# Start addresses of a float32r matmul kernel's moving tiles, modulo 256 bytes

## What is computed

```python
def _ffn_half(h, g, shift, scale, gate, w_in, w_out):            # first block, d_ff = 2816
    a, b = jnp.split(_modnorm(h, g, shift, scale) @ w_in, 2, axis=-1)
    return h + 0.5 * gate * ((jax.nn.silu(a) * b) @ w_out)
...
q, k, v, g = _ret_project(u, w_in, rope)                         # retention: query, key, value, gate
...
def second_block(x, ...):                                        # two layers
        f = _swiglu(_rmsnorm_2(h, ff1_norm_pre[l]), ff1_w_gate[l], ff1_w_up[l], ff1_w_down[l])
        h = h + 0.5 * _rmsnorm_2(f, ff1_norm_post[l])
        m = _hybrid_mixer(_rmsnorm_2(h, mix_norm_pre[l]), w_in[l], ...)   # SSD, pooling, attention
        h = h + _rmsnorm_2(m, mix_norm_post[l])
        f = _swiglu(_rmsnorm_2(h, ff2_norm_pre[l]), ff2_w_gate[l], ff2_w_up[l], ff2_w_down[l])
        h = h + 0.5 * _rmsnorm_2(f, ff2_norm_post[l])
```

## The kernel before

| product | lines | columns | moving, block | distance |
|---|---|---|---|---|
| first block at 512 tokens | L1193 to L1195, L1201, L1202, L1208 | 512 | 128, 128 | 0 |
| its token halves | L1289, L1291, L1297, L1327 to L1329, L1193 to L1195 (Fourier output) | 256 | 128, 128 | 0 |
| query and gate of the retention | L1193 to L1195 | 256 | 128, 128 | 0 |
| values of the retention | L1224 | 256 | 64, 128 | 192 |
| Fourier products, retention output | L1818, L1831, L1193 to L1195 | 256 | 64, 128 | 192 |
| last feed-forward of the first block, second block | L1193 to L1195, L1201, L1202, L1208 | 256 | 64, 128 | 192 |
| attention values of the second block | L1224 | 256 | 64, 64 | 0 |
| pool columns of the second block | L1224 | 264 | 128, 160, 192 or 224, 64 | 64 to 160 |

## Time and profile before

### The profile page before, as it was taken

One profiled execution on the slowest core, in us unless ns is written; L12 is line 12 of the kernel. 1 busy time (PEld: TensorE's weight loads), 2 busy tenths in 40 slices (PEclk: granted clock), 3 DMA queues, 4 the chain that ended last, 5 costly groups with the idle time before them and its releaser, 6 DMA issues. The chain is left out here.

```text
span 2772.4 us, 45421 instructions
## 1 busy us (share of the span) xinstructions
PE 2693.6 (97%) x18884; PEld 2464.9 (89%) x18884; DVE 1700.0 (61%) x2148; ACT 1135.4 (41%) x1432; POOL 0.9 (0%) x13
## 2 busy tenths in 40 slices
PE   7999999999999999999999999999999999998998
PEld 5878898878889888899998999999889999997998
DVE  6774655776325753444456655766877666587764
ACT  5222234522224222235245544544555454454543
POOL 0000000000000000000000000000000000000000
PEclk9999999999999999999999999999999999999999
DMA  8653631466233663544222566575526656652563
GB/s 271 210 182 113 191 111 61 143 185 190 88 95 109 197 195 121 175 136 130 86 92 92 183 193 190 167 221 173 153 77 197 188 168 197 191 168 76 166 180 126
DMA packets 377437, 428.86 MB, mean 155 GB/s; under 512 B 14016, under 2 KB 359488, under 8 KB 377152
## 3 DMA queue, kind: packets, MB, share of 16 engines
q1 hardware_dynamic: 376416, 424.79, 49.9%
q10 hardware_dynamic: 864, 1.80, 0.2%
HBM read 425.49 MB, written 1.05 MB: 154 GB/s over the span
## 5 line engine op out<-in xcount | busy, mean ns | idle before, releaser
L736 DVE TENSOR_TENSOR w_lo<-raw,w_hi 128x1024 fp32r<-128x1024 f32 (+1 forms) x672 | 798.8, 1198 | 806.3 <-ACT w_hi L727 799.5
L727 ACT ACTIVATE w_hi<-raw 128x1024 fp32r<-128x1024 f32 (+1 forms) x672 | 691.1, 1036 | 1018.8 <-PE ps L1195 839.7
L1193 PE MATMUL ps<-u_hi,w_hi 128*128 128x256 f32 (+1 forms) x3168 | 1000.8, 316 | 9.4 <-DVE tmp L1137 4.0
L1195 PE MATMUL ps<-u_hi,w_lo 128*128 128x256 f32 (+1 forms) x3168 | 994.6, 314 | 0.0
L1194 PE MATMUL ps<-u_lo,w_hi 128*128 128x256 f32 (+1 forms) x3168 | 994.6, 314 | 0.0
L1193 PEld LDWEIGHTS ps<-u_hi,w_hi 128*128 128x128 f32 x3168 | 597.3, 189 | 61.0 <-issue 15.8
L1195 PEld LDWEIGHTS ps<-u_hi,w_lo 128*128 128x128 f32 x3168 | 595.9, 188 | 40.6
L1194 PEld LDWEIGHTS ps<-u_lo,w_hi 128*128 128x128 f32 x3168 | 595.9, 188 | 39.3
L1193 PE MATMUL ps<-g_hi,w_hi 128*128 128x256 f32 (+1 forms) x1276 | 398.2, 312 | 0.0
L1195 PE MATMUL ps<-g_hi,w_lo 128*128 128x256 f32 (+1 forms) x1276 | 397.8, 312 | 0.0
L1194 PE MATMUL ps<-g_lo,w_hi 128*128 128x256 f32 (+1 forms) x1276 | 397.8, 312 | 0.0
(11 more groups left out here) (298 smaller groups left out, 2820.3 us busy)
## 6 DMA issues: line engine op xcount, KB each, us to landing
raw<-in_ffn_w_in SPq DMA_DIRECT2D x176, 512.0 KB, 4.4
raw<-in_w_mod SPq DMA_DIRECT2D x128, 512.0 KB, 4.3
raw<-in_ff_w_gate SPq DMA_DIRECT2D x88, 512.0 KB, 4.1
raw<-in_ff_w_up SPq DMA_DIRECT2D x88, 512.0 KB, 4.3
raw<-in_ffn_w_out SPq DMA_DIRECT2D x64, 512.0 KB, 3.4
raw<-in_ff_w_down SPq DMA_DIRECT2D x64, 512.0 KB, 3.5
raw<-in_ret_w_in SPq DMA_DIRECT2D x48, 512.0 KB, 3.6
raw<-in_w_in SPq DMA_DIRECT2D x36, 512.0 KB, 3.9
```

Source lines behind the costliest of these rows:

```text
L727: act.activation(w_hi[:, slot, unit_at(g, cols)], raw[:, raw_slot, 0:cols], ACT.Copy).then_inc(hi_ready, 1)
L736: dve.tensor_tensor(w_lo[:, slot, at], raw[:, raw_slot, 0:cols], w_hi[:, slot, at].bitcast(f32), ALU.subtract).then_inc(lo_ready, 1)
L1193: pe.matmul(out, w_hi[:, slot, cols], hi, start=first, stop=False, **check)
L1195: return pe.matmul(out, w_lo[:, slot, cols], hi, start=False, stop=last, **check)
```

## The change

All of `u_hi`, `u_lo`, `g_hi`, `g_lo` and the Fourier tables `dft_hi`, `dft_lo` (and with them `ab_hi`, `ab_lo`) now lie 192 bytes further on as a whole, whatever the number of tokens, and `tokens_at` adds nothing. In tokens mode the streamed weights are shifted by `W_SHIFT` = 32 elements (128 bytes) instead of 192 bytes, since the loaded tokens now start at 64. `ride_in_g`, which lies behind `g_hi`, moves along by 192 bytes.

```diff
-SHIFT, ROOM = 48, 64
+SHIFT, W_SHIFT, ROOM = 48, 32, 64
...
-        u_hi, u_lo = [x[:, 0:DT * NTOK].rearrange("p (k n) -> p k n", n=NTOK) for x in (u_hi_flat, u_lo_flat)]
+        u_hi, u_lo = [x[:, SHIFT:SHIFT + DT * NTOK].rearrange("p (k n) -> p k n", n=NTOK) for x in (u_hi_flat, u_lo_flat)]
...
-        _, g_hi, g_lo = overlay([("g_room", [P, 16], f32), ("g_hi", [P, FT, NTOK], f32r),
+        _, g_hi, g_lo = overlay([("g_room", [P, 16 + SHIFT], f32), ("g_hi", [P, FT, NTOK], f32r),
                                  ("g_lo", [P, FT, NTOK], f32r)])
-        _, ride_in_g = overlay([("before_ride", [P, 16 + FT * NTOK + (FT - 8) * NTOK], f32),
+        _, ride_in_g = overlay([("before_ride", [P, 16 + SHIFT + FT * NTOK + (FT - 8) * NTOK], f32),
...
-            ("dft_room", [P, 5, SEQ], f32), ("dft_hi", [P, 5, SEQ], f32r), ("dft_lo", [P, 5, SEQ], f32r),
+            ("dft_room", [P, 5 * SEQ + SHIFT], f32), ("dft_hi", [P, 5, SEQ], f32r), ("dft_lo", [P, 5, SEQ], f32r),
...
-        def tokens_at(n, wide=False):
-
-            at = SHIFT if n == SEQ and not wide else 0
-            return slice(at, at + n)
+        def tokens_at(n):
+
+            return slice(0, n)
...
-            at = SHIFT if g.mode == "tokens" and cols <= KT_MAX * UCOLS else 0
+            at = W_SHIFT if g.mode == "tokens" and cols <= KT_MAX * UCOLS else 0
...
-                return [x[:, k, tokens_at(g.tokens, g.more.get("both"))] for x in (u_hi, u_lo)]
+                return [x[:, k, tokens_at(g.tokens)] for x in (u_hi, u_lo)]
```

## The result

| | before | after |
|---|---|---|
| median, us | 2781.09 | 2806.45 |
| lowest, highest | 2773.3, 2790.4 | 2801.65, 2812.04 |
| the profiled execution | 2774.21 | 2806.45 |
| its span | 2772.4 | 2804.6 |
| PE busy, PEld busy | 2693.6, 2464.9 | 2728.1, 2471.3 |

The change is slower: ratio 1.0082, 95% interval 1.0059 to 1.0104 (five runs of each). The forecast was 2769 us with a range of 2740 to 2790, and slower by over 0.5% had a chance of 0.07.

A forecast was written before the change was run, and what follows sets the result against it. TensorE was taken as the bound, its cost set by matmul start intervals. About 12 us gained at 256 columns and 0 at 512 gave 2762 from the profiled 2774.2, or 2769 us against the 2781.1 median; full range 2740 to 2790.

The forecast's parts named there:

- Price of the second set: 4356 matmuls of 512 columns, moving-tile start minus block start going from 0 to 192 bytes: taken as 0 us.
- the lower bound: 512-column streams lose their regular rhythm, 232 ns against 227: 5.3 ns x 4356 = 23 us lost.
- Price of the first set: 2232 matmuls of 256 columns, distance 0 to 192: 5.8 ns each, 12.9 us gained, two windows in ten at 117.8 ns.
- the gate: Gate stage, where TensorE waits 4.0 us for VectorE's `acc`: half of its 384 matmuls' 2.2 us counted as lost.
- Rival 2: First block's 512-column streams (L1193 to L1195) stay at 232 ns: 23 us lost, 2792 us; sign 88 per 20 us; chance 0.13.
- Rival 1: Distance 0 costs every load 6.7 ns, at 512 columns too: 25 us more gained, 2744 us; chance 0.13.
- rival 3: Distance does nothing and the 120 ns belong to something else in those stages: time stays at 2781 us; chance 0.08.
- Other edits at nothing: `ride_in_g` moved by 192 bytes, VectorE and ScalarE work, and products staying at distance 192, retention values included: 0 us.
- more than 3 windows in 10 at 172: Second block's 20 us windows turning to 172 matmuls: over 4 us lost at no fault of the change.
- The signs: Per 20 us, query product 179 matmuls instead of 169, 512 columns still 90; L1327 and L1289 276 to 281 ns, not 283.

The follow-up runs named there:

- the streams alone: Kernel of matmuls alone, one fixed distance per stream: 512 columns 226.7 ns at distance 0, 233.3 at 192; 256 columns 120.0, and 113.3 or 117.8.
- second pair of profiles: The kernel before and the changed kernel, each unchanged, profiled once more: spans 2775.4 and 2794.0 us; the changed kernel's median 2795.76 us, ratio 1.0074.

## Why the prediction was wrong

- **"Price of the second set" failed.** I took 0 for 4356 matmuls of 512 columns between +29 us and -23. Measured: 27.6/4356 = 6.3 ns lost for each (233.3 against 226.7 in steady stretches, one unit of 6.67), beyond the lower bound. Both rows behind the 0 were misread. The single 256-column start after a 512-column stretch says nothing of steady prices: in the streams alone the first four intervals of L56 were 112 to 119 ns, and it settled at 120.0. And a load of 188 ns is no sign of an undisturbed stream: at 512 columns it is 188 at 226.7 and at 233.3 alike.
- **The bound itself was weak.** The 23 us came from a transient (232 ns in the earlier trace rows) and were exceeded by 4.6. The same transient stands at distance 0 in the streams alone, where the first five intervals of L48 were 228 to 236 ns before it settled at 226.7: it is how such a stream settles, and tells nothing of distance 192. No row had 512 columns at 192, and the taken value rested on inference from another width and from one start; the range should have reached further to the slow side.
- **Price of the first set: mechanism right, size too large.** 12.9 us, less 1.1 for the gate, were forecast. The excess of the 2232 moved matmuls fell from 14.1 to 4.8 us, 9.3/2232 = 4.2 ns each and not 5.8, and in the second pair of profiles by 9.5. The share at 117.8 ns was 0.2 in my sum; stretch by stretch it is about 0.4 in the changed kernel (some 900 of the 2232). The query window shows it: 174 matmuls, not 179.
- **Rival 2 was right in place and sign**, at a chance of 0.13: the 512-column streams keep a longer interval. It was a little small: with 5.3 ns and the full gain it gave 2792. That reads meet at another point of the stream, its reason, no run shows. With the measured sums it gives 2781 + 27.6 - 9.5 = 2799, between the two medians of the changed kernel, 2806.45 and 2795.76. Its own threshold, slower from 6 ns on, was passed.
- **Rival 1 and rival 3 fell.** The 34 units of 512 columns hold nothing that a new distance takes away; no stream fell under 226.7. And distance does matter. The Trainium skill (TensorE: Matmul & The Clock Gate, "What happens when you issue a matmul") states independent read ports for the moving data and the weights. By that rule the eight distances would cost the same. With matmuls alone on the chip they cost 113.3 to 120.0 and 226.7 to 234.2 ns.
- **"Other edits at nothing" held** where a row can tell: the sums on `ride_in_g` are in flight for 391 ns as before, and the gate stage's wait is 4.2 us for 4.0. The retention's values, with the pair changed from 64 on 128 to 0 on 64, had 0.9 us of excess before, 0.1 and 0.5 after, a change of the size of a draw.
- **The unchanged stages were a chance I had named** (more than 3 windows in 10 at 172). The first profile had 6.8 us of it, the second 0.1 against its own before.
- **The signs.** Under 512 columns a window holds 87, where 88 was the sign of rival 2. The groups of L1327 and L1289 came to 282 and 281 ns, just outside the 276 to 281 and at its edge; the 283 that they were to fall from was misread, since the earlier trace rows have 287 and 286 for them.

Not shown: why these pairs cost what they do. The unit of 16 cycles and the dependence on both starts fit reads that meet in memory, but no run here separates that from another cause.

## What to carry to other kernels

A rule about addresses belongs to one tile shape. Before extending it to other widths, time it with matmuls alone, in streams of 40 matmuls or more, from several entries, with the pair of starts and not only their difference. And where a kernel's runs scatter by 20 us with no wait to blame, look whether equal streams show two prices: a different pair of starts may remove the scatter and the time.

## What was not expected of the hardware

- A steady float32r stream's interval depends on the moving tile's start and the block's start. At 256 columns it ran from 113.3 to 122 ns, at 512 from 226.7 to 234.2, and the good pairs of the two widths are different.
- Shifting both tiles by the same amount can matter: 512 columns at 120 on 120 cost 233.3, at 128 on 128 226.7.
- 256 columns at 0 on 64, and at 64 on 128 in the kernels, have two stable prices, 113.3 and 117.8 ns. A program of matmuls alone fell into the same ones in both its executions, the full kernel did not: 17.1 and 3.6 us of excess in two executions of one program.
- Streams of 128 and of 192 columns cost the same 111.6 ns, at distance 0 and at 192.
